# Sharing differential attention's weighted sum between VectorE and GpSimd, in a rebuilt attention loop without interleaved gate products

## The reference, cut to what matters

```python
# latent attention: k, v over 1280 keys for latent queries, over 256 for context queries (layer 0 only)
p = softmax(q @ k.T * 96 ** -0.5);  y = p @ v
# differential attention, head dimension 32
p = softmax(q1 @ k1.T * scale) - lam * softmax(q2 @ k2.T * scale);  y = rms_norm(p @ v) * (1 - lam_init)
# merge
term = sigmoid(h @ w_gate[l, i]) * ((branches[i] * silu_gates[i]) @ w_branch[l, i])
```

## Time and profile before

| | us |
|---|---|
| median of 3 runs | 4644.32 (4634.93 to 4653.32) |
| the profiled execution | 4637.01 |
| its span | 4635.2 |
| TensorE busy | 3676.0 (79%) |
| VectorE busy | 1965.0 (42%) |
| ScalarE busy | 1243.7 (27%) |
| GpSimd busy | 1066.2 (23%) |

### The profile page before, as it was taken

How to read it: one execution, slowest core, us unless ns; L and a number is a source line. 1 busy time by engine, 2 the same in 40 slices (tenths; PEclk the granted TensorE clock), 3 DMA queues, 4 the chain that set the end, 5 groups by cost and what they waited for, 6 DMA issues and landing times. The chain is left out here.

```text
span 4635.2 us, 63721 instructions
## 1 busy us (share of the span) xinstructions
PE 3676.0 (79%) x25724; PEld 2856.5 (62%) x25724; DVE 1965.0 (42%) x3281; ACT 1243.7 (27%) x2126; POOL 1066.2 (23%) x1114
## 2 busy tenths in 40 slices
PE   5987987466886999897776878987666879998677
PEld 2764656355675777786662665665455757776565
DVE  4224432455345555203553324432554355554255
ACT  2102321344122323213301202321443223232340
POOL 2001001322113343223401101102331034333250
PEclk7978988688898999998987889998788989999898
DMA  4101013100101111335634101014011121111472
GB/s 165 40 34 42 18 34 94 40 26 18 58 29 59 50 44 45 100 118 164 233 105 159 52 32 45 26 33 116 27 31 37 38 65 50 53 53 52 159 252 91
DMA packets 202584, 334.45 MB, mean 72 GB/s; under 512 B 22976, under 2 KB 96448, under 8 KB 200640
## 3 DMA queue, kind: packets, MB, share of 16 engines
q1 hardware_dynamic: 173504, 283.34, 19.3%
q10 hardware_dynamic: 28800, 47.20, 2.8%
HBM read 249.45 MB, written 81.00 MB: 71 GB/s over the span
## 5 line engine op out<-in xcount | busy, mean ns | idle before, releaser
L89 PE MATMUL ps<-hh,wh_ds 128*128 128x512 f32 (+1 forms) x1600 | 689.3, 431 | 79.9 <-POOL wl_ds L202 28.7
L90 PE MATMUL ps<-hl,wh_ds 128*128 128x512 f32 (+1 forms) x1600 | 617.3, 386 | 0.0
L91 PE MATMUL ps<-hh,wl_ds 128*128 128x512 f32 (+1 forms) x1600 | 616.2, 385 | 0.0
L89 PEld LDWEIGHTS ps<-hh,wh_ds 128*128 128x128 f32 x1600 | 322.0, 201 | 161.3 <-issue 54.7
L90 PEld LDWEIGHTS ps<-hl,wh_ds 128*128 128x128 f32 x1600 | 322.3, 201 | 58.5 <-issue 16.7
L91 PEld LDWEIGHTS ps<-hh,wl_ds 128*128 128x128 f32 x1600 | 319.6, 200 | 58.5
L1060 DVE TENSOR_REDUCE mx_d<-ps 128x1 f32<-128x1280 f32 (+1 forms) x144 | 197.2, 1369 | 252.6 <-PE ps L979 252.5
L200 POOL CAST wh_ds<-raw_ds 128x512 fp32r<-128x512 f32 x160 | 107.8, 674 | 792.4 <-DMA raw_ds<-in_d_wmerge 309.2
L933 PE MATMUL ps<-const,qk_da 128*128 128x128 f32 x656 | 131.3, 323 | 163.3 <-ACT pt_da L1101 161.1
L2009 DVE TENSOR_TENSOR T_dr<-T_dr,ps 64x256 f32<-64x256 f32 x400 | 167.6, 419 | 200.3 <-PE ps L1765 191.0
L1131 ACT ACTIVATE qk_da<-ps,nmx_d 128x1280 f32<-128x1280 f32 (+1 forms) x144 | 177.4, 1232 | 229.2 <-DVE nmx_d L1062 229.1
(11 more groups left out here) (322 smaller groups left out, 7977.1 us busy)
## 6 DMA issues: line engine op xcount, KB each, us to landing
gate_sums<-out_ds ACTq DMA_DIRECT2D x160, 256.0 KB, 2.0
raw_ds<-in_d_wmerge SPq DMA_DIRECT2D x128, 256.0 KB, 2.7
logit_mg<-gate_sums SPq DMA_DIRECT2D x128, 256.0 KB, 3.4
w_mod<-in_d_wmod SPq DMA_DIRECT2D x12, 2048.0 KB, 19.7
R_dr<-decay_rows SPq DMA_DIRECT2D x80, 256.0 KB, 4.4
qk_da<-turned_qk SPq DMA_DIRECT2D x32, 320.0 KB, 7.1
q_raw_da<-turned_qk SPq DMA_DIRECT2D x288, 32.0 KB, 1.8
acc_ou<-merged SPq DMA_DIRECT2D x18, 512.0 KB, 5.2
```

Source lines behind the costliest of these rows:

```text
L89: pe.matmul(out, w_hi, x_hi, start=first, stop=False)
L90: pe.matmul(out, w_hi, x_lo, start=False, stop=False)
L91: return pe.matmul(out, w_lo, x_hi, start=False, stop=last)
```

## The change

- The attention loop carries no gate products: `plan`, `load`, `tensor`, `cut`, `move` and `spot` are gone from it. The plans of the other stages stay, so those chunks are made later.
- The three groups of transposes are 4, 2 and 4 blocks; the middle one has a place of its own in bank 7. The first turn comes after the last score piece of map 0 (one map: after piece 1), the second after the last of map 1, the third directly behind. `value` follows the last score piece of map 0 (one map: piece 1) of even heads.
- The maximum is written negated, with no scaling behind it; the scale is put on q before (GpSimd while staging with one map; ScalarE in `prepare_maps` with two, before q is stored). The sum of map 0 goes straight to `tot`.
- With one map VectorE makes its two moves ahead of the maximum.
- With two maps `q_raw` has two buffers and `qs` two slots.
- In the long differential stage the weighted sum is shared by keys: VectorE forms columns 0 to 767 in one instruction, GpSimd columns 768 to 1279 in two (scale, add), queued behind the staging of the unit two ahead. The third turn and the exponential of map 0 wait for it as well.

The diff, cut to its core:

```diff
-        limit = min(self.upto(point), max(self.start, self.end - 2 * KD))
+        low = self.start if self.end > self.start else 0
+        limit = min(self.upto(point), max(low, self.end - 2 * KD))
...
-    groups = [(at, min(4, key_tiles - at)) for at in range(0, key_tiles, 4)]
+    groups = [(0, 4), (4, 2), (6, 4)] if key_tiles == NT else [(0, CT)]
...
+    SL = 2 // maps
+    near = 768 if maps == 2 and key_tiles == NT else keys
+    value_at = pieces[-1][0] if maps == 2 or len(pieces) == 1 else pieces[-2][0]
...
-    fill = m.dense
-    fill.plan((n_tiles - 1) * SPOTS, KD // SPOTS, (7,))
     with ExitStack() as st:
         sb = lambda n, s, d=F32: st.enter_context(nc.sbuf_tensor(f"{n}_{name}{l}_{t0}", s, d))
...
-            def turn_bank(count):
-                return m.ps[:, 6, 0:count * P]
+            def turn_bank(g, count):
+
+                return m.ps[:, 7, BR:BR + count * P] if g == 1 else m.ps[:, 6, 0:count * P]
 
...
+                        if g >= 2:
+                            sp.wait_ge(staged, 2 * (g - 1))
                         at = 2 * (h % 2)
                         src = m.d_qk[:, h // 2, cols(i)].rearrange("(j r) c -> r j c", r=ROPE)[:, at:at + 2]
...
-                            sp.dma_start(q_raw[ROPE * a:ROPE * a + ROPE], src).then_inc(q_in, 16)
-                    fill.load(sp, SPOTS * (i - 1))
+                            sp.dma_start(q_raw[ROPE * a:ROPE * a + ROPE, g % 2], src).then_inc(q_in[g % 2], 16)
...
+                def stage(g):
+                    if maps == 1:
+                        if g >= HEADS:
+                            pool.wait_ge(scored, g - HEADS + 1)
+                        slot, src = q_part(g % HEADS, g // HEADS + t0)
+                        pool.tensor_scalar(slot, src, QK ** -0.5, None, ALU.mult).then_inc(staged, 1)
+                        return
+                    pool.wait_ge(q_in[g % 2], 64 * (g // 2 + 1))
+                    if g >= 2:
+                        pool.wait_ge(scored, 2 * (g - 1))
+                    raw = q_raw[:, g % 2]
+                    pool.tensor_copy(qs[:, g % 2], raw).then_inc(q_high, 1)
+                    pool.wait_ge(q_high, g + 1)
+                    for rows in (slice(ROPE, 2 * ROPE), slice(3 * ROPE, 4 * ROPE)):
+                        pool.tensor_tensor(qs[rows, g % 2], raw[rows], qs[rows, g % 2].bitcast(F32), ALU.subtract
+                                           ).then_inc(staged, 1)
+                    pool.wait_ge(staged, 2 * (g + 1))
+
+                def mix(u):
+
+                    h = u % HEADS
+                    pool.wait_ge(inverse, u + 1)
+                    rest = e[:, h % 2, 1, near:keys]
+                    pool.tensor_scalar(rest, rest, mx[:, h:h + 1], None, ALU.mult).then_inc(weighted, 1)
+                    pool.wait_ge(weighted, u + 1)
+                    pool.tensor_tensor(rest, rest, e[:, h % 2, 0, near:keys], ALU.add).then_inc(mixed_far, 1)
+
+                units = n_tiles * HEADS
+                for g in range(units):
+                    stage(g)
+                    if near < keys and g >= 2:
+                        mix(g - 2)
+                if near < keys:
+                    for u in range(units - 2, units):
+                        mix(u)
...
-                    last = u * G + g - 1
-                    if last >= 0:
-                        movers, moved = (on_act, moved_a) if last % G in on_act else (on_dve, moved_d)
-                        pe.wait_ge(moved, last // G * len(movers) + movers.index(last % G) + 1)
+                        if near < keys and g == 2:
+                            pe.wait_ge(mixed_far, u + 1)
+                    if g != 1 and (g == 2 or u):
+                        back, g_last = (0, 0) if g == 2 else (1, G - 1)
+                        movers, moved = (on_act, moved_a) if g_last in on_act else (on_dve, moved_d)
+                        pe.wait_ge(moved, (u - back) * len(movers) + (movers.index(g_last) + 1))
+                    if g == 1 and h == 0:
+                        pe.wait_ge(y_done, i + 1)
+                    elif g == 1:
+                        movers, moved = (on_act, moved_a) if g in on_act else (on_dve, moved_d)
+                        pe.wait_ge(moved, (u - 1) * len(movers) + (movers.index(g) + 1))
...
+                        pe.wait_ge(staged, maps * (u + 1))
+                        g = 0
                         for a in range(maps):
-                            n = (i * HEADS + h) * maps + a
-                            if a == 0:
-                                pe.wait_ge(staged, maps * (i * HEADS + h + 1))
-                            if n >= 2:
-                                pe.wait_ge(exp_done, n - 1)
-                            for x, (at, width) in enumerate(pieces):
-                                mm = pe.matmul(scores(h, a)[:, at:at + width],
-                                               qs[:, h] if maps == 1 else qs[:, (i * HEADS + h) % 3, a],
+                            if u >= SL:
+                                pe.wait_ge(exp_done, (u - SL) * maps + (a + 1))
+                            for at, width in pieces:
+                                mm = pe.matmul(scores(h, a)[:, at:at + width], qs[:, h] if maps == 1 else qs[:, u % 2, a],
                                                k_all(h, a)[:, at:at + width], start=True, stop=True)
-                                if x == len(pieces) - 1:
+                                if at + width == keys:
                                     mm.then_inc(scored, 1)
-                                if h == 2 and i and a == 0 and x == 0:
-                                    value(i - 1, 0)
-                                if x == len(pieces) - 1 and a == 0:
-                                    if h == 3 and i < n_tiles - 1:
-                                        spot(i, 1)
-                                    if h == 0 and i:
-                                        spot(i - 1, 2)
-                                    if h == 1 and i:
-                                        spot(i - 1, 3 if maps == 2 else 4)
-                                if before:
-                                    for g in turns.get(x + a * len(pieces), ()) if G > 1 else ():
-                                        turn(*before, g)
-                            if before and G == 1 and a == maps - 1:
-                                turn(*before, 0)
-                            if h == 1 and i and a == 1:
-                                spot(i - 1, 4)
-                        if h == 2 and i:
-                            value(i - 1, 1)
+                                if a == 0 and i and h % 2 == 0 and at == value_at:
+                                    value(i - 1, h // 2)
+                                if before and g < G and (at + width == keys or maps == 1 and at >= value_at):
+                                    turn(*before, g)
+                                    g += 1
+                        while before and g < G:
+                            turn(*before, g)
+                            g += 1
                 i = n_tiles - 1
                 for h in range(HEADS - LAG, HEADS):
...
+                    if h % 2 == 0:
+                        value(i, h - HEADS + LAG)
                     for g in range(G):
                         turn(i, h, g)
-                    value(i, h - HEADS + LAG)
+                value(i, PAIRS - 1)
 
             @block.vector
...
                     dve.wait_ge(inverse, u + 1)
-                    dve.scalar_tensor_tensor(out=e[:, h % 2, 1], in0=e[:, h % 2, 1], scalar=mx[:, h, 1:2],
-                                             in1=e[:, h % 2, 0], op0=ALU.mult, op1=ALU.add).then_inc(mixed, 1)
+                    dve.scalar_tensor_tensor(out=e[:, h % 2, 1, 0:near], in0=e[:, h % 2, 1, 0:near], scalar=mx[:, h:h + 1],
+                                             in1=e[:, h % 2, 0, 0:near], op0=ALU.mult, op1=ALU.add).then_inc(mixed, 1)
 
                 def find(n, h, a):
 
                     dve.wait_ge(scored, n + 1)
-                    dve.reduce_max(mx[:, h, a:a + 1], scores(h, a), AX.X).then_inc(dve_step, 1)
-                    dve.wait_ge(dve_step, n + 1)
-                    dve.tensor_scalar(nmx[:, h, a:a + 1], mx[:, h, a:a + 1], -scale, None, ALU.mult).then_inc(maximum, 1)
+                    dve.reduce_max(nmx[:, h, a:a + 1], scores(h, a), AX.X, negate=True).then_inc(maximum, 1)
...
+                        if maps == 1 and i and h == LAG:
                             finish(i - 1)
                         if before:
-                            move(*before, on_dve[:1])
+                            move(*before, on_dve)
+                            if maps == 1:
+                                invert(before[1])
+                        if maps == 1 and i and h == LAG - 1:
+                            keep(i - 1)
                         for a in range(maps):
```

(23 more changed lines are left out.)

95 lines of the change are left out of this document (27 added, 68 removed).

## The result

The changed kernel takes 4415.72 us (median; 4412.32 to 4422.76), the kernel before 4645.48 us (4634.93 to 4653.32): ratio 0.9509, interval 0.9486 to 0.9532, 230 us less. The forecast was 4455 with a range of 4375 to 4545; it lay 39 us high. The profiled execution of the changed kernel took 4417.81 us with a span of 4416.0, against a span of 4635.2 before: -219.2 us.

What follows compares the result with a forecast made beforehand. Stages run one after another; TensorE was taken to bound gate products, a chain of waits differential attention, latent lying between. Terms -212 - 83 - 18 + 128 + 3 = -182 against 4637.0 us gave 4455, range 4375 to 4545.

Steps and rivals of the forecast that it cites:

- (5): Rival: sharing the mix gains nothing, differential unit 5.5 to 6.0 us, time near forecast; chance 0.60 together with the forecast.
- (b): Long differential stages: new order of turns and shared mix give 5.95 us a unit, stages 210 us, -109 and -103.
- (c): Long latent stages: 5.5 us a unit, 184 us each, -39 and -44, of which seven chunks 32 to 38.
- (a): Gate products leave attention for `apply_gates`: +62 and +66 us, +128 in sum, with shorter idle tails before the merge.
- The lock: Differential mix: the skill's exclusion rule would add 9 us in all; the prediction read a lock taken in turns.
- (d): Short tiles of layer 0: two q buffers overlap loading, differential -14 us; latent has one chunk less, -4.
- (e): Attention loops: removed scaling of the maximum and removed copy of the sums, counted inside the loops, no separate size.
- (f): `prepare_maps`: ScalarE scales q tiles and q is stored later, +3 us (0 to +8); GpSimd's latent q scaling 0.
- (2): Rival: differential attention stays at the lower clock or GpSimd's queue adds a microsecond, 7.0 us a unit, 4522; chance 0.19.
- (3): Rival: everything meets its bound, 5.2 us a differential and 5.0 a latent unit, 4375 us; chance 0.12.
- (4): Rival: GpSimd bounds differential attention, scores wait for its staging, 9.5 us a unit at longest times, 4682; chance 0.05.

Runs made afterwards that it cites:

- e5_old_order: Changed kernel with the first turn back ahead of the last score piece and ScalarE's last move behind map 1's exponential, in long differential stages: 4590.42 us.
- e4_before_no_fill: Kernel before with the gate products taken out of attention alone, all 30 chunks computed in the gate stages: 4693.52 us.
- e3_tt_scale: Changed kernel with GpSimd's scaling written as a product of two tensors, factor spread with stride 0: 4398.19 us.
- e8_latent_one_bank: Changed kernel with the three turns of a latent unit in one bank again, differential stages untouched: 4486.21 us.
- e12_one_q: Changed kernel with each load of q held until the unit before is staged, as one q buffer would do: 4460.46 us.
- e1_whole_mix: Changed kernel with VectorE mixing all 1280 columns and GpSimd only staging q: 4396.56 us.
- e2_far256: Changed kernel with the mix split at 1024, GpSimd taking 256 columns in place of 512: 4387.71 us.

## Why the prediction was right, and where not

The time came out within the range, 39 us below the forecast. The prediction gave one chance to its forecast and to rival (5) together; by the runs it is (5) that came, the sharing of the mix gains nothing. That the total came so near is in part luck, since errors in (b) and in (c) stand against each other. By its steps:

**(a) Gate products, +128.** Measured +60 and +70. A chunk still leaves each 5.44 us (moves at 4104.75 and 4110.19), and the idle time ahead of the merge is 11.0 and 21.4 us where 12 and 22 were forecast:

```profile
2018.67 0.58 PE L89 MATMUL ps<-yh_mg,wh_ds 128*128 128x256 f32 x1 [11.00 <-DVE wl_ds L2237]
...
4169.59 0.80 PE L89 MATMUL ps<-yh_mg,wh_ds 128*128 128x512 f32 x1 [21.36 <-DVE wl_ds L2237]
```

**(b) Differential attention, -212; measured -243.** The mechanism of the order was right: e5_old_order brings back move, turn and score piece, and 88 of the 104 and 109 us by which the changed stages are shorter than those of e4_before_no_fill. Two sizes were off, in opposite directions. The scaling on GpSimd was taken at 0.65 us, with bounds of 0.61 and 1.28 (the cast of 512 columns and the two-input form). It took 1.56, beyond both bounds: the form with a pointer is dearer than the cast (0.61), than the add (1.27) and than the same product written with two tensors (1.04 in e3_tt_scale):

```profile
L912 POOL TENSOR_SCALAR qk_da<-qk_da,mx_d x64: 1562/1563/2383, 812.6 to 3249.0; 128x512 f32<-128x512 f32 x64
```

So GpSimd's unit is 5.55 and not 5.0 to 5.4, and it, not VectorE's loop of 5.1 to 5.2, sets the stage. The other way, the forecast had added 0.5 us for each unit with values, 2% of slips, and a third of the time at the lower clock. Value products fit into TensorE's waits for the staging (the unit from 904.00 to 909.55 has them and is 5.55 us long like the next), and the clock was 0.88 and 0.90: with levels of 1 and 0.5 of full speed that is a quarter or less of the time at 1.2 GHz. 5.95 a unit was forecast, 5.5 came.

**The lock.** The prediction weighed, where mix and subtractions were both stretched, against the Trainium skill, "SBUF — State Buffer", section "Who interferes with whom": a VectorE instruction with two SBUF inputs and a GpSimd instruction that reads SBUF exclude each other. The traces side with the skill: the mix of 1.02 us is untouched and the scaling of 2.31 does nearly all of its work when it has ended. The earlier trace rows fit it too: it is two subtractions and one mix, the mix waited 0.55 us, and the pair ended 0.59 us behind it, so one subtraction of 0.72 went ahead and one came after. In layer 0 the mix took 1.19 us on average for 1.02 (ten of 32 took 1.4 to 1.6), so the forecast's 0.5 us on VectorE was 0.17. Its 1.0 us on GpSimd was 0.65: 0.21 on the scaling, 0.44 on the pair of subtractions (1.88 for 1.44).

**(c) Latent attention, -83; measured -99.** The sum was near, the split wrong. The prediction gave 32 to 38 us a stage to the seven chunks and said that the rebuild gives little. By e4_before_no_fill the chunks are 29 and 34 and the rebuild 18 and 18; by e8_latent_one_bank the second bank is worth 31, and without it the rest of the rebuild is 13 us slower than the old order (206.9 against 194.4). Which part of the rest costs that, VectorE's moves ahead of its maximum or another, was not tried. I had costed the third turn's wait for the first move at 0.3 us a unit and not asked what it saves that the second waits for none.

**(d) Short stages, -18.** Measured -18 and about -2 (forecast -14 and -4); the mechanism of the first is shown by e12_one_q. **(e), (f)** and all else: +3 forecast, some +13 measured. The 8.2 us around `prepare_maps` in layer 1 are not ScalarE's scaling of q, which (f) priced: e4_before_no_fill lacks this scaling and has the same 153.7 us there. They came with the chunks' removal; how is open.

**The rivals.** (2), 7.0 us a unit, did not come; the clock rose as gaps closed. (3) was near for latent attention (5.25 a unit against its bound of 5.0). (4), GpSimd as the bound, has the mechanism right and the size wrong: the unit is 5.55 us a unit, far from the 8.8 from which it would have decided. I had set it against the sum at long durations only and not asked what it does at the medians plus the one duration that no row showed. (5), that the sharing gains nothing, came and worse: it costs 17 and 16 us a stage. Its reason was another than the prediction gave, GpSimd's queue and not a loop of maxima and exponentials.

What the change is made of: chunks out of attention +46 (e4_before_no_fill against before); then, against e4_before_no_fill, the differential long stages -104 and -109, of which the order of turns and moves is 88 and 89 and the rest (second bank, buffers, shared mix) 16 and 20; the latent rebuild -18 twice; the short differential stage -18. That is -221, where the two profiled spans differ by 219. The pieces don't add in general: the second bank alone is worth 35 us a stage once the order is new.

## What to carry to other kernels

When work is shared with a second engine, add up that engine's whole queue per unit, with what else it must deliver, and price each operand form by a row of just that form; where none exists, leave room above the dearest neighbour (1.28 us here, against 1.56 measured) and don't take the cheapest. Work that an idle engine carries at a quarter to half of its price inside a slow loop can cost its full price once the loop is tight, so test such fillings again after each shortening. Turns and moves that hand one bank back and forth make both engines wait, so ask what stands behind each of the two waits.

## What the runs showed of the hardware

- GpSimd, 128x512 fp32 in place: scaling by a pointer 1.56 us, add of two tensors 1.27, product with a factor spread with stride 0 1.04 (e3_tt_scale), cast to fp32r 0.61. With a constant factor a scaling of 96x128 takes 0.52:

```profile
L894 POOL TENSOR_SCALAR qs_la<-q_la x72: 524/524/528, 422.9 to 2876.6; 96x128 f32<-96x128 f32 x72
```

- A GpSimd instruction that starts during VectorE's two-input mix waits for its end, also the small cast: 0.92 and 1.27 us in place of 0.40 in e1_whole_mix, each ending 0.26 us behind a mix of 1.55. In all three forms some 0.13 us less than the instruction's own time is left behind the mix (0.26 of 0.40, 0.90 of 1.04, 1.43 of 1.56). It goes the other way as well: a mix took 1.90 us for 1.02 beside a scaling of 1.04.
- TensorE's granted clock in the long differential stage of layer 0 was higher in each shorter version without chunks: 0.69 in e4_before_no_fill (182 us busy of 300), 0.75 in e5_old_order (168 of 284), 0.88 after (145 of 196), 0.93 in e2_far256 (133 of 175). The 40 products of a pair of heads take 2.40 us at the upper level and 4.01 us in e5_old_order's unit above.
